# Experts 0 and 7 of the first mixture moved into TensorE's loops, and two weight blocks asked for later

## The reference, cut to what matters

```python
logits = (x2 @ w_router).astype(jnp.float32) + b_router.astype(jnp.float32)
top_vals, top_idx = lax.top_k(logits, TOP_K)
gates = jax.nn.softmax(top_vals, axis=-1)
...
def expert_block(args):
    xb, e = args
    h = xb @ w_in[e]                                   # 1024 -> 2 x 2816
    return (jax.nn.silu(h[:, :D_FF]) * h[:, D_FF:]) @ w_out[e]   # 2816 -> 1024
...
y = jnp.zeros_like(x2).at[slot_tok].add((ys * slot_gate[:, None]).astype(x2.dtype))
```

## Time and profile before

| | us |
|---|---|
| median of three runs | 1942.84 (1938.73 to 1943.52) |
| the profiled execution | 1936.89 |
| its span, first to last instruction | 1935.1 |
| TensorE busy / weight loads busy | 1781.0 / 1401.6 |
| VectorE, ScalarE, GpSimd busy | 519.9, 251.2, 159.6 |
| mixture, from the first step f = 0 to the last block | 534.0 to 1254.1 |

### The profile page before, as it was taken

One profiled execution on the slowest core, in us unless ns is written; L12 is line 12 of the kernel. 1 busy time (PEld: TensorE's weight loads), 2 busy tenths in 40 slices (PEclk: granted clock), 3 DMA queues, 4 the chain that ended last, 5 costly groups with the idle time before them and its releaser, 6 DMA issues.

```text
span 1935.1 us, 52713 instructions
## 1 busy us (share of the span) xinstructions
PE 1781.0 (92%) x24496; PEld 1401.6 (72%) x24496; DVE 519.9 (27%) x1239; ACT 251.2 (13%) x657; POOL 159.6 (8%) x307
## 2 busy tenths in 40 slices
PE   8999999999988999999999999889989999989775
PEld 7758885567588988988898989777757778653331
DVE  2641000224311111110101010146774443242223
ACT  2320000033101000000000000022232112010000
POOL 0000000100007400000000000055430000000000
PEclk9999999999999999999999999989989999999988
DMA  8224433331397999999999999941301028579996
GB/s 322 98 95 183 170 135 148 138 147 44 123 402 314 369 375 401 385 416 360 395 384 389 388 394 399 403 142 32 110 26 64 35 77 367 201 315 427 427 426 275
DMA packets 62952, 498.30 MB, mean 258 GB/s; under 512 B 7096, under 2 KB 15824, under 8 KB 17104
## 3 DMA queue, kind: packets, MB, share of 16 engines
q1 hardware_dynamic: 52672, 490.11, 63.0%
q10 hardware_dynamic: 10128, 5.97, 1.1%
HBM read 494.99 MB, written 1.05 MB: 256 GB/s over the span
## 4 chain that ended last, share of the span: by engine, by line
PE 75%; DMA 17%; DVE 4%; issue 2%; ACT 1%; ACTq 1%; DVEq 0%; SPq 0%
PE pb L1162 12%; PE pb L806 11%; PE pb L1193 10%; DMA ringbuf<-in_ein 10%; PE pb L815 7%; PE pb L811 4%; PE pb L879 3%; PE pb L1064 3%; DMA ringbuf<-in_e2out 2%; PE pb L1407 2%; PE pb L1384 2%; PE pb L1673 2%; DMA arena<-in_e2in 2%; PE pb L1109 2%; DMA ringbuf<-in_e2in 2%
## 5 line engine op out<-in xcount | busy, mean ns | idle before, releaser
L1162 PE MATMUL pb<-arena,ringbuf 128*64 128x80 f32 x11264 | 421.8, 234 | 27.3 <-issue 10.6
L1162 PEld LDWEIGHTS pb<-arena,ringbuf 128*64 128x64 f32 x11264 | 403.4, 138 | 45.3 <-issue 31.8
L1735 DVE TENSOR_TENSOR arena<-arena,pb 128x160 f32<-128x160 f32 (+3 forms) x130 | 48.0, 369 | 647.5 <-ACT arena L2704 402.3
L1193 PE MATMUL pb<-arena,ringbuf 128*64 128x80 f32 x5632 | 202.7, 233 | 16.9 <-issue 16.5
L1193 PEld LDWEIGHTS pb<-arena,ringbuf 128*64 128x64 f32 x5632 | 197.7, 137 | 22.1 <-issue 21.5
L806 PE MATMUL pb<-XT,ringbuf 128*128 128x256 f32 (+2 forms) x1104 | 201.9, 345 | 0.8 <-ACT XT L2504 0.8
L806 PEld LDWEIGHTS pb<-XT,ringbuf 128*128 128x128 f32 (+1 forms) x1104 | 180.3, 192 | 22.1 <-issue 2.1
L2504 ACT ACTIVATE arena<-pb 128x256 f32<-128x256 f32 (+5 forms) x188 | 72.8, 405 | 541.5 <-PE pb L1193 182.6
L815 PE MATMUL pb<-arena 64*64 64x64 f32 (+4 forms) x664 | 106.1, 322 | 6.0 <-DVE Y L1735 3.5
L815 PEld LDWEIGHTS pb<-arena 64*64 64x64 f32 (+4 forms) x664 | 51.8, 152 | 56.4 <-issue 28.6
L811 PE MATMUL pb<-ringbuf,arena 128*128 128x512 f32 x192 | 83.6, 593 | 2.9 <-DVE arena L1735 1.8
(11 more groups left out here) (391 smaller groups left out, 1799.6 us busy)
## 6 DMA issues: line engine op xcount, KB each, us to landing
ringbuf<-in_ein SPq DMA_DIRECT2D x176, 1024.0 KB, 7.4
ringbuf<-in_eout SPq DMA_DIRECT2D x64, 1408.0 KB, 9.7
arena<-in_e2in SPq DMA_DIRECT2D x13, 2048.0 KB, 26.6
ringbuf<-in_e2in SPq DMA_DIRECT2D x12, 2048.0 KB, 35.9
ringbuf<-in_fin SPq DMA_DIRECT2D x11, 2048.0 KB, 7.6
ringbuf<-in_e2out SPq DMA_DIRECT2D x8, 2048.0 KB, 31.3
ringbuf<-in_wo SPq DMA_DIRECT2D x6, 2048.0 KB, 7.8
arena<-in_e2out SPq DMA_DIRECT2D x6, 2048.0 KB, 34.2
```

The source lines that it names most:

```text
L1162: ins = pe.matmul(PB[4 + f % 2][h_, t * C1:(t + 1) * C1], w3[:, k, (t % 2) * 128 + h_.start:(t % 2) * 128 + h_.stop], XG[e % 2][:, k, :], ...
L1193: ins = pe.matmul(PB[d % 2][h_, 0:C1], w3[:, f, h_], HT[:, f, :], start=f == 0, stop=f == 21)
L1735: return v.tensor_tensor(o, a, b, op)
```

## The change

Three things. The loops take all experts: the signals `hnD`, `ytA` and `ytD` get a first entry "free" (signalled by VectorE's addition of the router's bias, by ScalarE's warming activation and by VectorE's scaling of X), so that the first waits of the loops have something to compare with. In expert 7 the first S5 set moves ahead of the scatter and the second one behind it, out of the eight blocks. And SP asks for only two blocks of in_eout at the entry, the other two with the rest of expert 0's.

```diff
-        hnD = sig("exp_hid", [(1, e, f) for e in E8 for f in range(11)] + [(2, q) for q in Q8])
+        hnD = sig("exp_hid", ["free"] + [(1, e, f) for e in E8 for f in range(11)] + [(2, q) for q in Q8])
...
-        ytA, ytD = [sig(n, [(e, i) for e in E8 for i in range(4)]) for n in ("yt_even", "yt_odd")]
+        ytA, ytD = [sig(n, ["free"] + [(e, i) for e in E8 for i in range(4)]) for n in ("yt_even", "yt_odd")]
...
-            def up_pair(e, i):
...
-            def up_pairs(e, first):
+            def up_pairs(e):
 
                 with pe.register(f"hid{e}") as hid:
-                    pe.reg_mov(hid, 11 * e + 2 * first)
-                    with pe.Fori(16 * (5 * e + first + 1), 16 * (5 * e + 6), 16) as landed:
+                    pe.reg_mov(hid, 11 * e + 1)
+                    with pe.Fori(16 * (5 * e + 1), 16 * (5 * e + 6), 16) as landed:
                         for f in (1, 2):
                             pe.wait_ge(hnD.sem, hid)
                             for x in range(2):
                                 pe.wait_ge(loop_in[in_slot(f, x)], landed)
                                 up_half(e, f, x).then_inc(inP.sem, 1)
                             pe.reg_add(hid, hid, 1)
...
-            def down_four(e, i):
...
-            def down_fours(e, first):
+            def down_fours(e):
 
                 with pe.register(f"read{e}") as read, pe.register(f"even{e}") as early:
-                    pe.reg_mov(read, 4 * e + 2 * first)
-                    pe.reg_mov(early, 16 * (2 * e + first + 1) + at_out)
-                    with pe.Fori(16 * (2 * e + first + 1), 16 * (2 * e + 3), 16) as landed:
+                    pe.reg_mov(read, 4 * e + 1)
+                    pe.reg_mov(early, 16 * (2 * e + 1) + at_out)
+                    with pe.Fori(16 * (2 * e + 1), 16 * (2 * e + 3), 16) as landed:
...
                     turn(e - 1)
-                else:
-                    up_pair(e, 0)
-                up_pairs(e, 0 if e else 1)
+                up_pairs(e)
+                if e == NE1 - 1:
+                    s5_turn(Z.rearrange("p k (q n) -> p (k q) n", q=4), [ysA.at((1, e - 1)), ysD.at((1, e - 1))], "z", btP)
                 if e:
                     scatter(1, e - 1, PGT, YS)
                 if e + 1 < NE1:
                     gather(1, e + 1, [ysA.at((1, e - 1)), ysD.at((1, e - 1))] if e else [pgA.at((1, 0)), xgD.at((1, 0, 1))], PS, PG, XG)
                 else:
-                    s5_turn(Z.rearrange("p k (q n) -> p (k q) n", q=4), [ysA.at((1, e - 1)), ysD.at((1, e - 1))], "z", btP)
+                    s5_turn(dup, [btA.at(0), btA.at(1)], "dup", ctP)
                 pe.wait_ge(*hnD.at((1, e, 10)))
-                if e == 0 or e == NE1 - 1:
-                    down_four(e, 0)
-                if e == 0 or e == NE1 - 1:
-                    down_four(e, 1)
-                else:
-                    down_fours(e, 0)
+                down_fours(e)
...
-                    for i in range(4):
+                    for i in range(2):
                         load_out(0, i)
...
-                for d in range(4 if e == 0 else 0, 8):
+                for d in range(2 if e == 0 else 0, 8):
                     load_out(e, d)
```

## The result

The changed kernel took 1921.37 us in the median of four runs (1920.61 to 1922.63), the kernel before 1940.78 beside it (1938.60 to 1943.52): ratio 0.9897 [0.9883, 0.9912], 19.4 us less. The prediction was 12.3 us less and 1930.5 us, with a range from 1923 to 1938.

The account below looks back on a forecast made before the run. TensorE, busy 92% of the span, was taken to bound the kernel, leaving its idle and slow time to win. Gains of 6.5 + 3.1 - 0.9 + 3.6 = 12.3 us bring 1942.84 to 1930.5 us, range 1923 to 1938.

Parts of the forecast that it names:

- The entry: Expert 0's upward half: with two in_eout blocks asked for later, the third chunk is no longer late; gain 6.5 us.
- The backlog sum: Entry: some 3.3 MB queued ahead of f = 2's chunk, 7.8 us at 424 GB/s; without two blocks 0.4 MB.
- Rival 1: Entry: the third chunk stays late and only the loops count, 6.7 us gained, 1936.1 us; chance 0.12.
- Expert 0's downward half: Put in the loop, its second four blocks run from code already there: 29.54 to 26.40 us, gain 3.1, bounds 2.0 and 4.5.
- Expert 1 gave back: Expert 1's upward half: expert 0's shorter half leaves its first chunks less time; cost 0.9 us, bounds 0 and 2.4.
- Expert 7: Turns moved and downward half looped: 35.82 us becomes 32.19, gain 3.6, bounds 2.5 and 5.1.
- experts 1 to 6 stay as they are: Looped downward halves of experts 1 to 6: no term in the forecast, so 0 us gained.
- The sum: Whole kernel: 6.5 + 3.1 - 0.9 + 3.6 = 12.3 us gained.
- Rival 3: All loops: moved code makes each backward branch refetch its body, 40 x 1.3 = 52 us, 1982.5 us; chance 0.03.
- Rivals 3 and 4: Rival 3, and the fourth: only added branches and entries cost, 6 x 1.3 = 8 us, 1938 us; chance 0.04.
- Rival 2: Expert 0's downward half: the postponed in_eout blocks land late, leaving 3.5 us gained, 1939.3 us; chance 0.06.
- The base: Forecast time: median 1942.84 us, 5.95 above the profiled run's 1936.89, less 12.3 gives 1930.5.

Follow-up runs that it names:

- loops_only: The kernel after (loops and S5 sets changed), but with four blocks of in_eout asked for at the entry as before; ratio 0.9919 to the kernel before.
- N = 16: The kernel after with 16 small matmuls jumped over at the start of TensorE's program, so later code lies elsewhere; ratio 0.9937 to the kernel before.
- N = 32: The kernel after with 32 small matmuls jumped over at the start of TensorE's program; ratio 0.9882 to the kernel before, 1921.3 us.
- N = 48: The kernel after with 48 small matmuls jumped over at the start of TensorE's program; ratio 0.9950 to the kernel before, 1932.2 us.
- light_out: The kernel after, loading only 352 of 2816 columns of each in_eout block of experts 1 to 7; ratio 0.9800 to the kernel before, 1901.37 us.

## Why the prediction was off

**The entry held.** The backlog sum of the queue gave a landing time of 5.8 us at the least, 7.4 taken; it was 8.17 on the chain. The wait of 4.32 us went and with it the low clock, and `loops_only` brought both back. Forecast 6.5, measured 5.8 in the first profiles, 7.2 in the means: right. Rival 1 is out.

**Expert 0's downward half: mechanism right, size too small.** I took 26.40 us, the mean of the looped halves of the earlier trace rows, and wrote the gain as a second pass saved. What failed is the step that priced the first pass by halves that run at a DMA share of 0.92. The earlier trace rows had 0.30 in this very stretch, and the half was to begin in it. It takes 24.40 us: 5.1 gained in place of 3.1. A part of that is luck of the place: at N = 16, 32 and 48 the looped half takes 26.6, 25.1 and 25.9 us, and in the means the gain is 4.3. My upper bound of 4.5, from the busy time of 25.00, was too low too: that column itself falls to 24.40 when the stalls go.

**Expert 1 gave back 2.4, not 0.9,** in the first pair, at the bound that I gave, but 1.1 in the means, near the 0.9. The mechanism is plausible and not shown.

**Expert 7: 3.4 for 3.6** (3.5 in the means). Right. The second S5 set stands between the scatter and the blocks without a wait:

```profile
1207.44 3.79 PE L815 MATMUL pb<-arena 80*128 80x512 f32 x8
1211.06 1.04 PE L1153 MATMUL pb<-cst,arena 128*128 128x128 f32 x8
1212.03 3.95 PE L1184 MATMUL pb<-arena,ringbuf 128*64 128x80 f32 x107
```

**That experts 1 to 6 stay as they are failed.** The sum has no term for their downward halves, and the prediction gives no reason for that. The removed code moved every loop, and their downward halves gained 2.9 us in the first profiles, 1.9 in the means. That it came out as a gain was luck: other places of the same code are up to 11 us slower. Rival 3 had the same cause with the other sign and a wrong mechanism: nearly all stalls of a looped downward half lie in its first pass, and what they cost depends on place and on the DMA. At the backward branch, behind record 352, no half of the kernel after has a gap over 0.15 us; the kernel before has 0.2 to 0.35 there in three of its six, against the 1.3 of the rival. Rivals 3 and 4 are out by the 704 matmuls without a gap. The rule of the Trainium skill on taken branches, cited there, does not bind for these bodies: two passes of a looped downward half in `light_out` take 24.40 us, 34.7 ns for each of 704 matmuls.

**Rival 2 is out**: the postponed blocks took 10.4 to 13.3 us to land against 18.5 of cover, and TensorE never waited for in_eout.

**The base.** The rest of the miss is no stage of the mixture. The profiled time fell by 16.3 us (1936.89 to 1920.61) where 12.3 stood, 4.0 us. But the time was also off by 5.2: I carried the 5.95 us between the profiled run (1936.89) and the median (1942.84) over to the changed kernel, whose profiled run, 1920.61, lies only 0.8 below its median. 4.0 and 5.2 are the 9.2 us between 1930.54 and 1921.37. The profile of before was simply a quick run, its timed runs range from 1934.8 to 1952, and rows of a quick run show too little of what there is to gain: the spans of five profiles before and six after differ by 18.7 us. Of these the terms of the sum make 13.9 (12.3 forecast), the looped halves of experts 1 to 6 1.9, and stretches that were put at nothing 2.9, 1.6 of it ahead of the mixture, whose start varies by up to 9 us between profiles of the kernel before alone.

**What stays open**: what sets the length of a stall at a given record (behind record 244 of expert 2's half 1.4 to 2.0 us in the kernels whose code lies like that of the kernel after, 127 records earlier 0.3 to 0.7), whether the code's transfers wait in line or are held up otherwise, and why the start of the mixture varies between 534 and 543 us in profiles of programs that are alike up to there.

## What to carry to other kernels

Before new code is priced, written out or looped, look at the DMA's share in the very stretch in which it is first run, and finer than by the pass: here a first pass of four blocks costs nothing while little is moved (0.18 in `light_out`), 0 to 2.2 us by its place at a mean share of 0.7, and 1.5 us in the mean in the looped halves of the kernel after. So loops pay most where weights stream. An edit worth under 1% that changes the length of a program is judged at several places of the code (a jump over N unused instructions sets them), since the place alone moved this kernel by 0.6%. A chunk that is late at an entry is best explained by summing the bytes asked for ahead of it, and one profiled run gives no offset to a median.

## What was not expected of the hardware

- Stalls of kind "issue" in new code come with the weight traffic: 9.1 us in six halves at a share of 0.92, none at 0.54, with the same code at the same place. They stand 127 matmul records, some 256 instructions, apart, or twice that.
- Unused instructions ahead of the code moved the time by 11 us (1921.3 us at N = 32, 1932.2 at N = 48).
- 96 matmuls of 8 columns took 20.65 us, 215 ns each, at the start of the program; the 16 of 128 columns behind them took 3.65 us, 228 ns each. Cutting the columns made that filler hardly cheaper.
